# First shift and scale in four column groups of TensorE, with the lagged output matrices moved into the first projection

## What is computed

```
cs = silu(c)                                   # 1024 values
shift, scale, gate = split(cs @ w + b, 3)      # w: 1024 x 3072, "thirds" of 1024 x 1024
h = x * (1 + scale) + shift                    # input of the first mixer
z = h @ w_in                                   # 448 columns: q part, kv part, rope part
q, k, v = norm(z) @ w_qb, norm(z) @ w_kvb      # 8 heads, rotary on 64 of 192 columns
o = causal softmax attention(q, k, v) @ w_o    # then x = layer_norm(ALPHA * x + gate * o)
```

## Time and profile before

| | |
|---|---|
| median of 3 runs | 1801.37 us (1799.45 to 1803.9) |
| the profiled execution | 1798.16 us, its span 1796.2 us |
| granted TensorE clock over the span | 0.959 of 2.4 GHz |
| busy share of the span | PE 92%, DVE 63%, ACT 46%, POOL 8% |
| the chain that ended last, by engine | PE 70%, DVE 16%, ACT 5%, DMA 2%, POOL 2%, SP 1% |

### The profile page before, as it was taken

How to read it: one execution, slowest core, us unless ns; L and a number is a source line. 1 busy time by engine, 2 the same in 40 slices (tenths; PEclk the granted TensorE clock), 3 DMA queues, 4 the chain that set the end, 5 groups by cost and what they waited for, 6 DMA issues and landing times.

```text
span 1796.2 us, 20549 instructions
## 1 busy us (share of the span) xinstructions
PE 1660.3 (92%) x8247; PEld 1339.6 (75%) x8247; DVE 1139.6 (63%) x1346; ACT 835.0 (46%) x1129; POOL 150.2 (8%) x293
## 2 busy tenths in 40 slices
PE   8777899987989899999999859999999999799998
PEld 3645688865668688878888747888888888678887
DVE  1786867796989856485556757454655456655454
ACT  2443455544225455553434775433644444654443
POOL 4230010006621010000000000000000000000000
PEclk9877999997999899999999979999999999899999
DMA  9658468873029376546654625555546555236552
GB/s 301 237 177 236 164 219 314 290 255 118 1 78 335 127 246 246 171 139 206 223 188 164 223 70 188 187 188 188 182 157 217 182 194 191 96 99 215 183 192 85
DMA packets 165497, 335.45 MB, mean 187 GB/s; under 512 B 38773, under 2 KB 54462, under 8 KB 164251
## 3 DMA queue, kind: packets, MB, share of 16 engines
q1 hardware_dynamic: 144602, 292.63, 48.3%
q0 software_dynamic: 9696, 37.29, 5.7%
q10 hardware_dynamic: 11104, 4.23, 0.9%
HBM read 328.86 MB, written 6.83 MB: 187 GB/s over the span
## 4 chain that ended last, share of the span: by engine, by line
PE 70%; DVE 16%; ACT 5%; issue 3%; DMA 2%; POOL 2%; SPq 1%; DVEq 0%; ACTq 0%; POOLq 0%
PE ps L635 22%; PE ps L637 21%; PE ps L636 21%; DVE wlo L1715 2%; PE ps L720 2%; ACT whi L1186 1%; PE ps L1157 1%; SPq L532 1%; DVE xlo L1720 1%; PE ps L714 1%; DMA raw<-in_mlp_w 1%; DVE G L1829 1%; DMA work<-in_mod_mix_w 1%; DVE G L1830 1%; DVE work L2150 1%
## 5 line engine op out<-in xcount | busy, mean ns | idle before, releaser
L1715 DVE TENSOR_TENSOR wlo<-raw,whi 128x2048 fp32r<-128x2048 f32 (+2 forms) x247 | 559.5, 2285 | 267.4 <-ACT whi L1186 267.1
L1186 ACT ACTIVATE whi<-raw 128x2048 fp32r<-128x2048 f32 (+2 forms) x247 | 466.5, 1907 | 230.8 <-PE ps L637 185.8
L635 PE MATMUL ps<-whi,xhi 128*128 128x512 f32 (+2 forms) x1244 | 478.9, 385 | 21.4 <-DVE xlo L1720 21.4
L637 PE MATMUL ps<-whi,xlo 128*128 128x512 f32 (+2 forms) x1244 | 473.3, 380 | 0.0
L636 PE MATMUL ps<-wlo,xhi 128*128 128x512 f32 (+2 forms) x1244 | 473.2, 380 | 0.0
L635 PE MATMUL ps<-whi,hhi 128*128 128x512 f32 x736 | 295.0, 401 | 27.5 <-DVE hlo L1720 27.0
L637 PE MATMUL ps<-whi,hlo 128*128 128x512 f32 x736 | 289.3, 393 | 0.0
L636 PE MATMUL ps<-wlo,hhi 128*128 128x512 f32 x736 | 289.1, 393 | 0.0
L635 PEld LDWEIGHTS ps<-whi,xhi 128*128 128x128 f32 x1244 | 236.3, 190 | 66.9 <-DVE xlo L1720 25.0
L637 PEld LDWEIGHTS ps<-whi,xlo 128*128 128x128 f32 x1244 | 236.5, 190 | 44.3
L636 PEld LDWEIGHTS ps<-wlo,xhi 128*128 128x128 f32 x1244 | 236.6, 190 | 42.1
(11 more groups left out here) (347 smaller groups left out, 1602.6 us busy)
## 6 DMA issues: line engine op xcount, KB each, us to landing
raw<-in_mlp_w SPq DMA_DIRECT2D x64, 1024.0 KB, 5.3
raw<-in_ffn_w_gate SPq DMA_DIRECT2D x44, 1024.0 KB, 5.1
raw<-in_ffn_w_up SPq DMA_DIRECT2D x44, 1024.0 KB, 5.1
raw<-in_ffn_w_down SPq DMA_DIRECT2D x44, 1024.0 KB, 4.9
mod<-in_mod_ffn_w POOLq DMA_DIRECT2D x16, 1024.0 KB, 6.3
mod<-in_mod_mix_w POOLq DMA_DIRECT2D x12, 1024.0 KB, 6.3
work<-in_mod_mix_w SPq DMA_DIRECT2D x8, 1024.0 KB, 8.6
operands<-in_mod_ffn_w SPq DMA_DIRECT2D x8, 1024.0 KB, 8.1
```

The source lines that it names most:

```text
L635: pe.matmul(o, lh, rh, start=start, stop=False)
L637: return pe.matmul(o, ll, rh, start=False, stop=stop)
L1186: act.activation(whi[:, c % SPL, 0:n], raw[:, c % RAW, 0:n], ACT.Copy).then_inc(hi_done, 1)
L1715: dve.tensor_tensor(wlo[:, c % RAW, 0:n], raw[:, c % RAW, 0:n], whi[:, c % SPL, 0:n].bitcast(F32), ALU.subtract).then_inc(lo_done, 1)
```

## The change

`first_thirds` copies the partial sums of the four column groups out of banks 4 to 7, divided by 32: those of the shift when chunk 3 is used, those of the scale when chunk 7 is. A matmul with the matrix of ones adds the 128 rows. Of `output_lag`, which takes a part number now, parts 0 to 4 hold two, one, one, one and one of the six operations. The diff, cut to its core:

```diff
@@ SP
+        mod_row = [operands[0:1, D * n:D * (n + 1)] for n in range(2)]
...
                 sp.dma_start(m0[n % 4], w0[:, 2 * kk:2 * kk + 2, D * third:D * (third + 1)]).then_inc(m0_in[n % 4], 16)
+                if n == 7:
+                    line(0)
                 if n == 5:
-                    line(0)
-                if n == 6:
                     sp.dma_start(X[:, :, :], t["x"][0].rearrange("(t p) d -> p t d", p=P)).then_inc(x_in, 16)
@@ PE, mla
                 turn("mla", 0)
+                pe.wait_ge(s5_in, 16 * 18)
+                pe.wait_ge(h_ready, 4)
+                for q in range(4):
+                    s5_turn(c_pad, q, q)
                 z_pass(0, 0)
...
                 z_pass(1, 1)
-                pe.wait_ge(s5_in, 16 * 18)
-                for q, b in enumerate((1, 2, 3, 6)):
-                    s5_turn(c_pad, q, b)
@@ PE, start
-            for b, half_row in enumerate(halves(GA, 2) + halves(BA, 2)):
-                pe.matmul(ps[:, b, :], ones[0:1, :], half_row[0:1, :], start=True, stop=False)
...
-                for hf in range(2):
-                    for k in range(2):
-                        last = pe.matmul(ps[:, 2 * third + hf, :], csB[:, 2 * kk + k, :], m0[n % 4][:, k, 512 * hf:512 * (hf + 1)],
-                                         start=False, stop=(kk == 3 and k == 1))
+                for k in range(2):
+                    for hf in range(2):
+                        a = 32 * ((2 * k + hf + kk) % 4)
+                        last = pe.matmul(ps[a:a + 32, 4 + 2 * third + hf, :], csB[:, 2 * kk + k, 0:32], m0[n % 4][:, k, 512 * hf:512 * (hf + 1)],
+                                         start=(kk < 2), stop=(kk >= 2))
+                if n < 4:
+                    last.then_inc(m0_used, 1)
+                elif n == 7:
+                    last.then_inc(m0_part, 1)
+                if n == 3:
+                    pe.matmul(ps[:, 0, :], ones[0:1, :], mod_row[0][:, 0:512], start=True, stop=False)
+                    pe.matmul(ps[:, 1, :], ones[0:1, :], mod_row[0][:, 512:], start=True, stop=False)
+                    pe.wait_ge(s5p_act, 1)
+                    pe.matmul(ps[:, 2, :], ones[0:1, :], mod_row[1][:, 0:512], start=True, stop=False)
+                    pe.matmul(ps[:, 3, :], ones[0:1, :], mod_row[1][:, 512:], start=True, stop=False)
-                if n == 4:
+                if n == 1:
                     pe.wait_ge(s5a_in, 48)
                     pe.wait_ge(s5p_pool, 1)
                     for k in range(3):
-                        last = pe.transpose(ps[:, 7, k * P:k * P + PAIRS], a_rows[:, k, :], ident[0:PAIRS, 0:PAIRS])
+                        last = pe.transpose(ps[:, 3, k * P:k * P + PAIRS], a_rows[:, k, :], ident[0:PAIRS, 0:PAIRS])
+            for third, r in enumerate((GA, BA)):
+                for hf in range(2):
+                    pe.wait_ge(m0_sum, 2 * third + hf + 1)
+                    last = pe.matmul(ps[:, 2 * third + hf, :], ones[:, :], r[:, 512 * hf:512 * (hf + 1)], start=False, stop=True)
@@ ACT
             x_hi("mla", 0)
             hi(1)
+            for q in range(4):
+                s5_matrix(q, q)
             x_hi("mla", 1)
...
-                for q, b in enumerate((1, 2, 3, 6)):
-                    s5_matrix(q, b)
                 hi(3)
@@ DVE, start
+            def first_thirds():
+                for third, r in enumerate((GA, BA)):
+                    if third:
+                        dve.wait_ge(m0_part, 1)
+                    else:
+                        dve.wait_ge(m0_used, 4)
+                    for hf in range(2):
+                        dve.tensor_scalar(r[:, 512 * hf:512 * (hf + 1)], ps[:, 4 + 2 * third + hf, :], 1 / 32, None, ALU.mult).then_inc(m0_sum, 1)
...
+            first_thirds()
+            lo(0)
             dve.wait_ge(s5p_pool, S5P_ANGLE)
             dve.reciprocal(g0v[:, 8, :], g0v[:, 8, :]).then_inc(s5p_dve, 1)
-            lo(0)
...
             x_lo("mla", 0)
             lo(1)
+            output_lag(0)
+            output_lag(1)
             x_lo("mla", 1)
@@ DVE, mla
                     dve.wait_ge(zn_ok, tt + 1)
+                    output_lag(2 + tt)
...
-                output_lag()
                 lo(4)
+                output_lag(4)
...
-                piece(0)
                 for g in range(2):
-                    if g:
-                        piece(1)
...
                 attention(0)
                 lo(8)
+                piece(9)
                 piece(10)
                 piece(11)
@@ DVE, attention
+                    if n == 0:
+                        if i in (4, 7):
+                            lo(6 if i == 4 else 7)
+                        else:
+                            piece(i if i < 4 else i - 1 if i < 7 else i - 2)
                     if i >= 3:
                         h, e = i - 3, HEADS * n + i - 3
                         dve.wait_ge(o_hi, e + 1)
                         rest(hlo[:, h, :], ps[:, 4 + h % 2, 0:L], hhi[:, h, :]).then_inc(o_ok, 1)
-                    if n == 0:
-                        if i in (4, 7):
-                            lo(6 if i == 4 else 7)
-                        elif i < 10:
-                            piece(i + 2 if i < 4 else i + 1 if i < 7 else i)
@@ POOL
-            for f in range(3):
-                open_third(f)
+            open_third(0)
             v = lambda k: g0v[:, k, :]
             pool.wait_ge(s5a_in, 48)
...
+            for f in (1, 2):
+                open_third(f)
```

More of the change, by code:

```diff
@@ L277, in build_program @@
         m0_in = [sem(f"m0_in{i}") for i in range(4)]
-        m0_used, m0_done, modb0_in, csb_ok = sem("m0_used"), sem("m0_done"), sem("modb0_in"), sem("csb_ok")
+        m0_used, m0_part, m0_sum, m0_done, modb0_in, csb_ok = sem("m0_used"), sem("m0_part"), sem("m0_sum"), sem("m0_done"), sem("modb0_in"), sem("csb_ok")
         piece_in = [sem(f"piece_in{i}") for i in range(9)]
@@ L579, in _ @@
             cols(craw, t["c"][0], c_in)
-            for n, r in enumerate((GA, BA)):
-                sp.dma_start(r[0:1, :], mod_b[0][D * n:D * (n + 1)].rearrange("(o n) -> o n", o=1)).then_inc(modb0_in, 16)
+            for n, r in enumerate(mod_row):
+                sp.dma_start(r, mod_b[0][D * n:D * (n + 1)].rearrange("(o n) -> o n", o=1)).then_inc(modb0_in, 16)
             with nc.allow_non_contiguous_dma(reason="short vectors"):
@@ L871, in mla @@
                 z_pass(1, 1)
-                pe.wait_ge(s5_in, 16 * 18)
-                for q, b in enumerate((1, 2, 3, 6)):
-                    s5_turn(c_pad, q, b)
+                pe.wait_ge(s5t_ok, 4)
                 for tt in range(T):
@@ L880, in mla @@
                 last.then_inc(zt_ps, 1)
-                pe.wait_ge(s5t_ok, 4)
                 chunk_ready(2)
@@ L1154, in _ @@
                 pe.wait_ge(m0_in[n % 4], 16 * (n // 4 + 1))
-                for hf in range(2):
-                    for k in range(2):
-                        last = pe.matmul(ps[:, 2 * third + hf, :], csB[:, 2 * kk + k, :], m0[n % 4][:, k, 512 * hf:512 * (hf + 1)],
-                                         start=False, stop=(kk == 3 and k == 1))
-                    if n == 7 and hf == 0:
-                        last.then_inc(m0_done, 1)
-                last.then_inc(m0_used if n < 7 else m0_done, 1)
-                if n == 4:
+                for k in range(2):
[14 more added lines that the diff above has]
+                if n == 1:
                     pe.wait_ge(s5a_in, 48)
@@ L1165, in _ @@
                     for k in range(3):
-                        last = pe.transpose(ps[:, 7, k * P:k * P + PAIRS], a_rows[:, k, :], ident[0:PAIRS, 0:PAIRS])
+                        last = pe.transpose(ps[:, 3, k * P:k * P + PAIRS], a_rows[:, k, :], ident[0:PAIRS, 0:PAIRS])
                     last.then_inc(s5p_ps, 1)
+            for third, r in enumerate((GA, BA)):
[3 more added lines that the diff above has]
+                    if third:
+                        last.then_inc(m0_done, 1)
             run = {"mla": mla, "s5": s5, "lru": lru, "kv": kv, "att": att}
@@ L1668, in _ @@
             for k in range(3):
-                last = act.activation(g0v[:, k, :], ps[:, 7, k * P:k * P + PAIRS], ACT.Copy)
+                last = act.activation(g0v[:, k, :], ps[:, 3, k * P:k * P + PAIRS], ACT.Copy)
             last.then_inc(s5p_act, 1)
@@ L2022, in mla, with output_lag @@
                 lo(8)
+                piece(9)
                 piece(10)
                 piece(11)
-            def output_lag():
-                dve.wait_ge(s5t_ok, 4)
-                dve.wait_ge(s5p_pool, 3)
+            def output_lag(part):
                 wide = lambda k: g0v[:, k, :].rearrange("p (m i o) -> p m i o", i=4, o=1).to_broadcast([P, KT, 4, 32])
@@ L2034, in output_lag @@
                 tmp = H[:, 0, :].rearrange("p (m i c) -> p m i c", m=KT, i=4)
[L2035 to L2041, removed]
+                if part == 0:
+                    dve.wait_ge(s5t_ok, 4)
```

(12 more changed lines are left out.)

1 line of the change is left out of this document (added).

## The result

The changed kernel takes 1844.34 us (median of four runs, 1840.48 to 1845.29) against 1802.53 us (four runs) for the kernel before on the same chip: a ratio of 1.023, 95% interval 1.021 to 1.0251. It is slower by 42 us. I had forecast 1806.0, with 1797 to 1813 as the range. The profiled execution has a span of 1838.4 us against 1796.2.

A forecast was written before the change was run, and what follows sets the result against it. PE carries 70% of the chain; the end of piece 5 was taken to set the first layer's end. 8.9 - 5.0 - 0.5 + 1.2 = +4.6 us on 1798.16 gives 1802.8; the median, 3.2 above, 1806.0; range 1797 to 1813.

The forecast's parts named there:

- part 1: Start: column groups shorten PE's chunk work, h begins at about 43 us; 0, between -3 and +3, slowed ACT loads included.
- the rival in which they take turns: Start: column groups run one after the other, h begins near 48.5 us, 1811.7 us in all; chance 0.06.
- half rate as the default until activity is sustained: Start: by the skill's rule PE stays at half clock, adding matmuls end near 45 us, 2 us late; not used in sum.
- Parts 2 and 3: Output matrices ahead of first pass, +0.7 (0 to +3); lagged matrices moved on DVE, V later by +1.15, the +0.7 included.
- Part 4: Between V copies and first scores: pieces 0 and 1 leave this stretch, -7.0 us.
- Part 5: Pieces in the attention: first scores to end of piece 5 takes 33.8 us instead of 19.0, +1.8 of it beside POOL.
- Part 6: From piece 5 to the output projection: last head stands behind piece 8, not 9, -5.0 us; chunk 9's weights and glue, -0.5.
- the end of piece 5 sets the end of the layer: First layer's end: behind piece 5 come 20.0 us of SP column loads, 7.0 us to piece 8's data, and the rest.
- Part 7: POOL's three fetches, 3 MB, start at about 147 us amid SP's column loads: +1.2 us, between 0 and +8.
- POOL's bulk holds the column loads back: Rival at the layer's end: SP's 20.0 us of column loads become 26 or more, +11, 1812 us; chance 0.18.
- The sum: First layer's end: 8.9 - 5.0 - 0.5 + 1.2 = +4.6 us, with the start taken as 0.

The follow-up runs named there:

- both moves: Changed kernel with the 18 loads of b and c issued by SP behind the first line, and SP's column loads between the fourth and fifth chunk: 1798.25 us, ratio 0.9968.
- the kernel with the matrices back: Changed kernel, b/c loads on SP, column loads early, c's loads behind the second line, output matrices in their old place: 1790.44 us, ratio 0.994, the fastest kernel.
- the kernels with h at 44 to 47 us: Changed kernel with the start as before: 1816.74 us; changed kernel with SP issuing chunk 4 only once b_re and b_im have landed: 1818.56 us.
- The moves of DMAs: Kernel before with b and c's 18 loads issued by SP behind chunk 7 and column loads between the fourth and fifth chunk: 1801.29 us, ratio 0.9992.

## Why the prediction was wrong, step by step

**The step that failed is in part 1: "if ACT's loads are slowed by the fuller rings, all of it slips with them, which is in the +3."** The mechanism was named and its price was not worked out. It was 28.4 us. ACT's end of issue came 28.7 us later than I had it (56.98 instead of 28.26), and h with it. That the way from there to h fits, 14.2 us against my 14.7, is luck: mine ended with the landing of the first line's weights, which was long past here. In its place PE's bias rows and four chunks took 9.4 us behind ACT's copies, and DVE's copies and `lo(0)` 3.4. The figure could have been read: I compared bulk alone (6 to 15 us) with bulk beside small packets (21 to 33) and took 344 against 394 GB/s for the price of sharing. The stretch between the two, 15 to 21 us at 168 GB/s with the engines busy, is the one in which b's packets moved, and it existed only because PE freed the place of chunk 0 so late, at 18.6 us. The change removed what held SP back; I counted that as a small gain.

**Right in part 1:** the column groups do overlap. Eight records of a chunk take 1.93 us at the lower of PE's two rates and 1.06 at the higher (fences below), against 3.70; the rival in which they take turns is out. Where DMA is ordered for it, h begins at 36.2, 6.6 us earlier, more than the 3 I gave as the best case.

PE's rate in that start (the first row of each fence is that of the stretches, its third number from the end the granted clock): with both moves the last chunk and the first two adding matmuls ran as in the first fence, in the kernel with the matrices back as in the second:

```profile
21.00:33.00 12.00, 10.42 (x37) 2.02 (x36) 1.29 (x2) 0.82 (x1) 4.98 (x22) 0.52 1.09 355
...
29.53 1.94 PE L1170 MATMUL ps<-work,wide_row 128*32 128x512 f32 x8 [0.64 <-DMA work<-in_mod_mix_w]
31.40 3.78 PE L1191 MATMUL ps<-GA,ones 128*128 128x512 f32 x4
```

```profile
21.00:33.00 12.00, 11.59 (x42) 3.01 (x41) 1.29 (x2) 0.81 (x1) 4.96 (x22) 0.67 1.09 354
...
29.53 1.06 PE L1169 MATMUL ps<-work,wide_row 128*32 128x512 f32 x8 [0.41 <-DMA work<-in_mod_mix_w]
30.53 1.98 PE L1190 MATMUL ps<-GA,ones 128*128 128x512 f32 x4
```

The same instructions, once at half the rate of the other; the granted clock of 21 to 33 us is 0.52 in the first kernel, all but the lower of its two levels (1.2 and 2.4 GHz), and 0.67 in the second. In the first PE had stood 0.94 us for chunk 6 and 0.64 for chunk 7; in the second it did three chunks on end in 5.29 us and stood 0.41. The Trainium skill (TensorE: Matmul & The Clock Gate, "Part 1: The HAM clock gate") has half rate as the default until activity is sustained, which I had set against the sum as 2 us. The first fence agrees with it (3.78 against 1.98, 1.8 us), the second does not stay there. h begins at 36.22 and 36.13: ahead of it `lo(0)` waits for ACT in both, so the clock decided nothing.

**Parts 2 and 3: right here.** h to V grew by 0.4 us against a forecast 1.15. But that holds only because c had landed before h, also in the kernels with h at 44 to 47 us. With the loads on SP and h at 36 us the same edit costs 7.1 us (43.3 against 36.2), over my upper end of +3 for part 2: I had not asked when c lands.

**Part 4: -7.0, measured -7.8.** Right.

**Part 5: 33.8 us, measured 39.6.** I gave one piece beside POOL, +1.8. Pieces 0 and 1 both were (2.2 us for each of their four operations, 1.28 alone): steps 0 and 1 took 5.7 and 6.7 us instead of 3.8 and 4.6. I took POOL's end as near the attention's start because before it is (106.6 against 104.4); with the scores 7.8 earlier relative to V, POOL ended at 137.6, 12.3 behind them. And ACT's next S5 matrix waits for POOL's memset of `wide_row`, with PE's scores behind it, so DVE stood 3.24 us. Sum: 1.9 + 2.1 + 3.2 - 1.8 + 0.5 in step 3 = 5.9 of the missing 5.8.

**Part 6: -5.5, and what stands behind the column loads took 6.8 less** (143.39 to 176.97 before, 192.27 to 219.07 after): right, and piece 8 stood ahead of the last remainder as forecast. But "the end of piece 5 sets the end of the layer" was too strong for the kernel before: without the column loads behind piece 5 its glue comes only 3.0 us sooner.

**Part 7: +1.2 taken, +7.4 measured** (26.9 against 19.6). The rival "POOL's bulk holds the column loads back" said 26 or more and had 0.18. The page it came from (DMA: Bandwidth & Descriptors, "Queues, rings and completion order", in the Trainium skill: an engine takes turns between its rings, a packet from each) pointed the right way. Its order of size is seen in five kernels here, 26.1 to 27.0 us. I did not bring the same rule to the start, where ACT's small packets meet SP's bulk. There the trace agrees with it to the packet, 1510 against 1509 from 21 to 33 us. Among the column loads it is not one for one, 1321 of SP's to 731 of POOL's from 176 to 184 us, but of the same kind.

**The sum:** +28.4 + 0.4 - 7.8 + 20.6 (39.6 against 19.0) + 7.4 - 6.8 = +42.2, the 42.1 of the glue and the 41.8 of the medians. Without the start it is +13.8 where I had +4.6.

## What to carry to other kernels

When an engine that paced a DMA queue gets faster, look for whoever lived in the pauses of that queue: list the transfers that landed while its rate was low, and price them as if the pauses were gone. Before moving deferrable work later, look up what its completion releases: here the places of the pieces were worth +10.3 or -2.0 us by whether thirteen column loads stood behind them. Work moved into an idle stretch inherits the due time of its inputs, and all that is queued behind it waits too.

## What the runs showed that I had not expected

An issue instruction can be the longest thing in a start: b_im's took 27.79 us beside full bulk, 26.23 us when it began 7 us later, 10.22 and 9.84 us with a hole in the bulk, 11.41 us on SP's own queue. ACT could compute nothing in that time.

The moves of DMAs that are worth nothing to the kernel before are part of one that beats it by 0.6%: whatever the column groups are worth shows only together with them. How much of the 0.6% is theirs was not measured: the kernel before with this order of the loads (the second line ahead of c) was not run. At V the fastest kernel is 7.7 us ahead of the kernel before, 6.7 of them since h; from V to the scores it gains 8.3, from there to the glue it loses 3.9.

At the very start the granted clock does not tell the rate of PE. In the fastest kernel the first two chunks take 1.94 us each, and their stretch shows 1.00; the fourth takes 1.06, and its stretch shows 0.81. The rows of the stretches and of the timeline:

```profile
0.00:15.00 15.00, 5.20 (x26) 1.02 (x27) 2.43 (x9) 5.88 (x18) 8.19 (x18) 1.00 0.76 266
15.00:21.00 6.00, 5.05 (x21) 1.58 (x14) 1.29 (x2) 0.86 (x2) 1.44 (x2) 0.81 1.03 408
...
8.93 1.94 PE L1169 MATMUL ps<-work,wide_row 128*32 128x512 f32 x8 [8.93 <-DMA work<-in_mod_mix_w]
11.53 1.94 PE L1169 MATMUL ps<-work,wide_row 128*32 128x512 f32 x8 [0.67 <-DMA work<-in_mod_mix_w]
...
16.68 1.06 PE L1169 MATMUL ps<-work,wide_row 128*32 128x512 f32 x8 [0.94 <-DMA work<-in_mod_mix_w]
```

Left open, besides: what the column groups do without the bias rows' move, where the pieces do best with the start of the fastest kernel, and whether its output matrices could still be lagged early once c is loaded sooner. None of these was tried.
